# Stage borders of a two-block fp32 network: half of the second weights split before the squares of x, and a K half of the first block computed by kinds of product

## The reference, cut to what matters

```python
def _rms_norm(x, g):
    y = x * lax.rsqrt(jnp.mean(x * x, axis=-1, keepdims=True) + EPS)
    return y * g
def _swiglu(x, w_gate, w_up, w_down):
    return (jax.nn.silu(x @ w_gate) * (x @ w_up)) @ w_down
def first_block(x, ...):
    for layer in range(2):
        hf = _swiglu(_rms_norm(x, g[0]), w_gate[layer, 0], w_up[layer, 0], w_down[layer, 0])
        x = x + 0.5 * _rms_norm(hf, g[1])
        mix = (_attn_mixer, _mlstm_mixer)[layer](_rms_norm(x, g[2]), ...)
        x = x + _rms_norm(mix, g[3])
        hf = _swiglu(_rms_norm(x, g[4]), w_gate[layer, 1], w_up[layer, 1], w_down[layer, 1])
        x = x + 0.5 * _rms_norm(hf, g[5])
    return x
def second_block(x, ...):
    for l in range(2):
        p = rms_norm(x, norm_g[l]) @ w_in[l]            # 1024 x 8776
        ...                                             # conv, sparse attention, pooling branches
        merged = g0 * y_a + g1 * y_b + g2 * y_c
        x = x + merged @ w_o[l]
    return x
```

## Time and profile before

| | |
|---|---|
| median of 3 runs | 1619.91 us (1619.64 to 1620.86) |
| the profiled execution, its time | 1618.21 us |
| its span in the trace | 1616.3 us |
| PE busy | 1573.8 us, 97% |
| DVE busy | 984.2 us, 61% |
| ACT busy | 815.7 us, 50% |
| granted TensorE clock | 1.0 of full speed |

### The profile page before, as it was taken

One profiled execution on the slowest core, in us unless ns is written; L12 is line 12 of the kernel. 1 busy time (PEld: TensorE's weight loads), 2 busy tenths in 40 slices (PEclk: granted clock), 3 DMA queues, 4 the chain that ended last, 5 costly groups with the idle time before them and its releaser, 6 DMA issues.

```text
span 1616.3 us, 19404 instructions
## 1 busy us (share of the span) xinstructions
PE 1573.8 (97%) x7499; PEld 1294.7 (80%) x7499; DVE 984.2 (61%) x1247; ACT 815.7 (50%) x1023; POOL 56.6 (3%) x99
## 2 busy tenths in 40 slices
PE   7999999899999999999999999999999999999999
PEld 6888877678888888887887888887778888777887
DVE  4555567765545654467666555557956665795664
ACT  5444456354444544357666444465365446636542
POOL 2000010000000000000000000011000000100000
PEclk9999999999999999999999999999999999999999
DMA  9654763155546554564436544664434456442443
GB/s 289 211 177 144 250 208 116 53 181 196 182 143 222 203 173 156 182 223 157 151 123 208 169 168 144 227 220 168 157 104 157 158 188 231 166 156 105 157 159 128
DMA packets 189093, 279.23 MB, mean 173 GB/s; under 512 B 8509, under 2 KB 102885, under 8 KB 189024
## 3 DMA queue, kind: packets, MB, share of 16 engines
q1 hardware_dynamic: 186752, 271.27, 48.4%
q0 software_dynamic: 2128, 6.97, 1.6%
q10 hardware_dynamic: 144, 0.03, 0.0%
HBM read 277.20 MB, written 1.06 MB: 172 GB/s over the span
## 4 chain that ended last, share of the span: by engine, by line
PE 71%; DVE 16%; ACT 7%; issue 3%; DMA 2%; POOL 0%; POOLq 0%; SPq 0%; DVEq 0%; ACTq 0%
PE ACC L778 20%; PE ACC L780 19%; PE ACC L779 19%; DVE WL L1984 6%; ACT WH L1348 2%; PE TB L809 2%; DVE WL L2293 1%; PE ZB L943 1%; DVE YC L2305 1%; DMA RAW<-ffn_w_down_in 1%; ACT XH L1379 1%; PE ACC L973 1%; PE ACC L975 1%; PE ACC L974 1%; DVE IS L2512 1%
## 5 line engine op out<-in xcount | busy, mean ns | idle before, releaser
L1984 DVE TENSOR_TENSOR WL<-RAW,WH 128x2048 fp32r<-128x2048 f32 (+2 forms) x256 | 507.7, 2026 | 262.8 <-ACT WH L1348 262.8
L778 PE MATMUL ACC<-WL,XH 128*128 128x512 f32 (+2 forms) x1312 | 516.2, 393 | 10.1 <-DVE WL L1984 5.3
L780 PE MATMUL ACC<-WH,XL 128*128 128x512 f32 (+2 forms) x1312 | 507.0, 386 | 0.0
L779 PE MATMUL ACC<-WH,XH 128*128 128x512 f32 (+2 forms) x1312 | 506.3, 386 | 0.0
L1348 ACT ACTIVATE WH<-RAW 128x2048 fp32r<-128x2048 f32 (+2 forms) x256 | 421.9, 1698 | 143.2 <-PE ACC L780 95.9
L778 PEld LDWEIGHTS ACC<-WL,XH 128*128 128x128 f32 x1312 | 247.1, 188 | 67.7 <-issue 9.6
L780 PEld LDWEIGHTS ACC<-WH,XL 128*128 128x128 f32 x1312 | 247.0, 188 | 50.6
L779 PEld LDWEIGHTS ACC<-WH,XH 128*128 128x128 f32 x1312 | 247.4, 189 | 46.3
L778 PE MATMUL ACC<-WL,HH 128*128 128x512 f32 x352 | 138.4, 393 | 1.4 <-DVE WL L1984 0.9
L780 PE MATMUL ACC<-WH,HL 128*128 128x512 f32 x352 | 137.1, 390 | 0.0
L779 PE MATMUL ACC<-WH,HH 128*128 128x512 f32 x352 | 137.1, 389 | 0.0
(11 more groups left out here) (316 smaller groups left out, 1807.1 us busy)
## 6 DMA issues: line engine op xcount, KB each, us to landing
RAW<-w_in_in SPq DMA_DIRECT2D x66, 1024.0 KB, 6.9
RAW<-ffn_w_gate_in SPq DMA_DIRECT2D x43, 1024.0 KB, 5.2
RAW<-ffn_w_up_in SPq DMA_DIRECT2D x43, 1024.0 KB, 7.4
RAW<-ffn_w_down_in SPq DMA_DIRECT2D x32, 512.0 KB, 4.5
RAW<-ffn_w_down_in SPq DMA_DIRECT2D x16, 1024.0 KB, 6.7
RAW<-mlstm_w_in_in SPq DMA_DIRECT2D x16, 1024.0 KB, 6.5
RAW<-ffn_w_down_in SPq DMA_DIRECT2D x16, 768.0 KB, 6.0
RAW<-attn_w_in_in SPq DMA_DIRECT2D x12, 1024.0 KB, 7.1
```

The source lines that it names most:

```text
L778: nc.tensor.matmul(bank, lh, wl[:, i, :], start=first and i == 0, stop=False)
L779: nc.tensor.matmul(bank, lh, wh[:, i, :], start=False, stop=False)
L780: mm = nc.tensor.matmul(bank, ll, wh[:, i, :], start=False, stop=last and i == k - 1)
L1984: nc.vector.tensor_tensor(WL[:, slot, lo:hi], RAW[:, slot, lo:hi], WH[:, slot, lo:hi].bitcast(F32), ALU.subtract).then_inc(lo_ready, 1)
```

## The change

Three edits. First, on PE, in the first block of every stage but the first, token tile 0: the second K half (K tiles 4 to 7) is no longer done K tile by K tile, but as four products `XH` by `WH`, then four `XH` by `WL`, then four `XL` by `WH`. Each kind has its own wait: `groups_hi` and `hi_ready`, then `lo_ready`, then `groups_used`. The transposes of token tile 1 now stand ahead of the last four. Second, on ACT, in every stage but the first, the first half of `WH` of the second chunk is made ahead of the squares and the second half right behind them; the table load of attn and mlstm comes after both, and the gate weights of mlstm ahead of all. Third, on DVE in attn, the copy to `BROW` goes ahead of `WL` of the second chunk. `at.rounded` on PE only counts groups for the new wait.

The diff, without the hunks that only add to `at.rounded` or only pass the new argument:

```diff
--- before.py
+++ after.py
@@ -759,7 +759,8 @@
                 wl = WL[:, slot, 0:k * n].rearrange("p (k n) -> p k n", k=k)
                 for tok in range(NTOK):
                     bank = acc_of(tok) if acc_of else ACC[:, block_odd * 2 + tok, 0:n]
-                    for i in range(k):
+                    high_first = fresh is not None and tok == 0 and at.stage > 0
+                    for i in range(k // 2 if high_first else k):
                         if fresh is not None and tok == 0 and i == k - 3:
                             of_x(1, fresh + 2)
                         if fresh is not None and i in (0, k // 2):
@@ -778,6 +779,20 @@
                         nc.tensor.matmul(bank, lh, wl[:, i, :], start=first and i == 0, stop=False)
                         nc.tensor.matmul(bank, lh, wh[:, i, :], start=False, stop=False)
                         mm = nc.tensor.matmul(bank, ll, wh[:, i, :], start=False, stop=last and i == k - 1)
+                    if high_first:
+                        t = slice(0, P)
+                        pe.wait_ge(hi_ready, 2 * chunk + 2)
+                        pe.wait_ge(groups_hi, at.rounded + 2)
+                        for i in range(k // 2, k):
+                            nc.tensor.matmul(bank, xh[:, i, t], wh[:, i, :], start=False, stop=False)
+                        pe.wait_ge(lo_ready, 2 * chunk + 2)
+                        for i in range(k // 2, k):
+                            nc.tensor.matmul(bank, xh[:, i, t], wl[:, i, :], start=False, stop=False)
+                        pe.wait_ge(groups_used, fresh + 3)
+                        for i in range(k // 2, k):
+                            if i == k - 4:
+                                of_x(1, fresh + 2)
+                            mm = nc.tensor.matmul(bank, xl[:, i, t], wh[:, i, :], start=False, stop=i == k - 1)
                     if tok == 0:
                         if last:
                             mm.then_inc(tile0_ready, 1)
@@ -826,6 +841,7 @@
                 product(XH, XL, at.chunk, at.chunk % 2, at.block, at.block % 2, 0, KD, n, True, True,
                         between=between, fresh=t)
                 at.group += 4
+                at.rounded += 4
                 at.stage += 1
             def next_x():
...
@@ -1338,19 +1358,19 @@
         def _(act):
             at = At()
-            def split_hi(c, slot, raw_wait, size):
+            def split_hi(c, slot, raw_wait, size, parts=(0, 1)):
                 k, n = size
-                act.wait_ge(raw_ready[slot], raw_wait)
-                if not (isinstance(c, int) and c == 0):
+                if 0 in parts:
+                    act.wait_ge(raw_ready[slot], raw_wait)
                     act.wait_ge(weights_used, c)
-                for lo, hi in ((0, k // 2 * n), (k // 2 * n, k * n)):
+                for lo, hi in [(part * (k // 2) * n, (part + 1) * (k // 2) * n) for part in parts]:
                     nc.scalar.activation(WH[:, slot, lo:hi], RAW[:, slot, lo:hi], ACT.Copy).then_inc(hi_ready, 1)
-            def split_next(size):
+            def split_next(size, parts=(0, 1)):
                 c = at.chunk + 1
                 if size:
-                    split_hi(c, c % 2, raw_value(c), size)
+                    split_hi(c, c % 2, raw_value(c), size, parts)
             def group_hi(bank_odd, ready, dst):
                 act.wait_ge(groups_ready, ready)
@@ -1381,7 +1401,7 @@
                     ins.then_inc(groups_hi, 1)
                     at.group += 1
-            def prenorm():
+            def prenorm(next_size, between=None):
                 if at.stage == 0:
                     for q in range(FIRST_PARTS):
@@ -1395,8 +1415,13 @@
                         nc.scalar.activation(WH[:, 0, cols], RAW[:, 0, cols], ACT.Copy)\
                             .then_inc(hi_ready if q % 2 else first_hi, 1)
                 x_hi(1)
+                if between:
+                    between()
+                ahead = (0,) if at.stage else ()
+                split_next(next_size, ahead)
                 for tok in range(NTOK):
                     square(X[:, tok, :], ST[:, :, :].rearrange("p t c -> p (t c)"), tok, 1)
+                split_next(next_size, (1,) if ahead else (0, 1))
                 at.stage += 1
                 at.rsqrt += 1
...
@@ -1502,9 +1526,8 @@
                 at.rsqrt += 2
             def attn(layer, next_size):
-                prenorm()
+                prenorm(FULL)
                 act.preload_act_table_set("natural_log_exp_and_others")
-                split_next(FULL)
                 wait_rx()
                 c0, b0, u0, g0 = at.chunk, at.block, at.unit, at.group + 1
                 staged_before = {1: 0, 3: 1, 4: 3}
@@ -1570,12 +1593,13 @@
                 out_product()
             def mlstm(layer, next_size):
-                prenorm()
+                def gate_hi():
+                    act.wait_ge(gate_weights, 16)
+                    nc.scalar.activation(GWH[:, :, :], GWR[:, :, :], ACT.Copy).then_inc(gate_weights_hi, 1)
+
+                prenorm(FULL, gate_hi)
                 act.preload_act_table_set("natural_log_exp_and_others")
                 at.ln += 1
-                act.wait_ge(gate_weights, 16)
-                nc.scalar.activation(GWH[:, :, :], GWR[:, :, :], ACT.Copy).then_inc(gate_weights_hi, 1)
-                split_next(FULL)
                 wait_rx()
                 c0, b0, u0, g0 = at.chunk, at.block, at.unit, at.group
                 staged_before = {1: 0, 3: 1, 4: 3}
@@ -1789,7 +1813,8 @@
                     at.block += 2
                 for b, kind in enumerate(ORDER):
-                    split_next(SIZES[b + 1])
+                    if b:
+                        split_next(SIZES[b + 1])
                     if kind == "out":
                         activations((2, 3))
                         out_tail()
@@ -2187,11 +2212,11 @@
             def attn(layer, next_size):
                 nc.vector.memset(VS[:, :, :, :, DH:DH + 1], 1.0)
                 prenorm()
-                split_next(FULL)
                 dve.wait_ge(groups_ready, at.group + 1)
                 nc.vector.tensor_copy(BROW[:, :], TB[at.group % 2][0:HEADS, 0:3 * P]).then_inc(bias_rows, 1)
                 dve.wait_ge(bias_rows, 1)
                 dve.sem_inc(groups_used, 1)
+                split_next(FULL)
                 c0, u0, g0 = at.chunk, at.unit, at.group + 1
                 def lo(j, half):
```

More of the change, by code:

```diff
@@ L894, in ffn @@
                 at.group += NGU
+                at.rounded += NGU
                 last_hidden = lambda: hidden((t0 + NGU - 1) % 2, t0 + NGU - 1, b0 + NGU - 1)
@@ L1047, in attn @@
                 at.unit += 2 * HEADS
+                at.rounded += KD // 2
                 at.chunk += 8
@@ L1696, in mix2 @@
             def mix2(layer, next_size):
-                prenorm()
+                prenorm(SIZES[1])
                 def skip(n):
```

## The result

| | before | with the change |
|---|---|---|
| median of 14 runs each | 1620.45 us (1619.52 to 1622.99) | 1623.85 us (1622.34 to 1625.03) |
| ratio of the runs, 95% interval | | 1.0020 (1.0013 to 1.0028) |
| the profiled execution | 1618.21 us, span 1616.3 us | 1623.34 us, span 1621.6 us |

The changed kernel is slower, by 3.2 us on the ratio (2.1 to 4.5). The forecast was +1.6 us: the right side, at half of the size. The median lies inside the wide range (1618.2 to 1624.4), but above the 1620.0 to 1623.1 that the forecast had called its own (0.5 us of that is the base, 1620.45 where 1619.91 had been shown). And 0.20% is just the bound of what it called no change. No work came in: each engine has as many instructions as in rows 1, and PE is busy for 1575.0 us, 1.2 us more, in a span that is 5.3 us longer. The rest is time in which PE stands.

What follows compares the result with a forecast made beforehand. PE, busy 97% of the span, was taken as the bound, with only 42.5 us of stops to win back. Seven border terms from -0.7 to +1.15 us summed to +1.6: 1619.9 + 1.6 = 1621.5 us, range 1618.2 to 1624.4.

Steps and rivals of the forecast that it cites:

- the sign and its reason: Five borders out of ffn or mix2: transposes five products later, so token tile 1 comes 1.15 us later; total +1.6 us.
- the order by kinds: attn to ffn and mlstm to ffn: 1.4 us of stops (0.98 + 0.42) move behind the transposes instead of going away.
- the half ahead of the squares: Second chunk's first `WL` half no longer ends a wait: -0.7 us at attn to ffn and mlstm to ffn, +0.44 at ffn to ffn.
- The cover of the second half: attn to ffn: second `WL` half ready on DVE at 354.2, needed at 354.7, a cover of 0.5 us.
- the bound that I had put at the end of its range: ffn to attn: forecast -0.5 us, bounded by -1.7 if all of 1.17 + 0.57 us came back.
- the step for mix2: Borders into mix2: `WL` of chunk 1 0.95 us later delays chunk 3's load; +1.05 us from ffn, +0.85 from mix2.
- the loads of mix2 slip more: Chunk 3, both mix2 stages: `WL` 2 us later, landing slips 2.85 us each, 1625.3 us; chance 0.12 with other lost covers.
- Two of the signs: In mix2, block 3 late by over 1.5 us would show it wrong; no `WL` stop starting any second block, right.
- the sharing of the loads: Borders into mix2: chunk 4's load shares the engines with chunk 3's, so chunk 3's landing slips by 0.75 us.
- my formula: Loads in mix2: a landing slips by twice its own delay less the other's, 2 x 0.95 - 1.15 = 0.75 us.
- Free transposes: Rival, at the borders: moved transposes cost nothing and all stops go, 5.8 us, giving 1614.1 us; chance 0.06.
- Absorbed in mix2: Rival: DVE stops PE again in mix2, the last two borders' +1.9 us goes, sum -0.3, 1619.6 us; chance 0.14.

Runs made afterwards that it cites:

- the split alone: Only the ACT and DVE edits (half of `WH` ahead of the squares, `BROW` ahead of `WL`), PE's order as before, against the kernel before: 1618.01 us, ratio 0.9985.
- the second profile: The kernel before, unchanged, profiled once more: 1621.2 us.
- the next: ACT and DVE edits with PE's order as before, DVE's wait for `RX` in mix2 behind the `WL` split of chunk 1, against the kernel before: 1615.03 us, ratio 0.9966.

## Why the prediction was right, and where it was not

**Right: the sign and its reason.** At four borders `XL` of token tile 1 already ended the wait, so moving the transposes by five products had to be paid. 1.15 us was forecast. The transposes come 1.10 us later at ffn to ffn, and the PE edit alone costs 1.13 to 1.19 us at four of the five borders and 0.99 at the last.

**Right: the order by kinds wins nothing** at attn to ffn and mlstm to ffn; at attn to ffn the stops of 0.98 and 0.42 us became 0.60 and 0.82.

**Right, a little small: the half ahead of the squares.** -0.92 and -0.77 against -0.7 forecast, +0.38 against +0.44. The cover of the second half (0.5 us) held in these stages. At ffn to attn it is -0.49 against -0.5: the split alone gives -1.70 there, the bound that I had put at the end of its range, and the transposes take 1.2 of it.

**Wrong: the step for mix2.** I had written that `WL` of chunk 1 waits for "a half of `WH` behind the squares: I get 0.95 later", and of `RX` that it is ready later but "still ahead of the take-out". The second was read on ACT only. DVE in mix2 has `wait_rx()` ahead of its first split (L2594 of the kernel before), which ffn and mlstm have behind theirs and attn does not have. In the kernel before this wait cost nothing, by 0.1 us: `RX` was complete at 1058.54, the first half of `WH` at 1058.64, and `WL` started at 1058.78. That is 0.14 us behind `WH`, as the view says; where `WH` alone holds it, with the `RX` wait moved, it starts 0.10 to 0.16 us behind. With half of `WH` ahead of the squares that half is early, and `RX` is late and takes its place.

The step counted the half of `WH` and put the wait for `RX` at nothing. With that wait moved behind, `WL` of chunk 1 is complete 0.79 and 0.78 us later than before, so the 0.95 was nearly right for what it counted. With the wait where it is, the delay was 2.26 and 2.18 us: 1.1 for the transposes and 1.1 for the half of `WH` that now stands ahead of the squares, from which `RX` is made. The two terms of the sum were 1.05 and 0.85 and measured 2.89 (2.03 against the second profile) and 2.07. That covers the gap between +1.6 and the measured time; the other five terms came out 0.34 us lower than forecast.

This is the place and nearly the slip of the rival "the loads of mix2 slip more", which had 0.12 and gave another reason, squares and read-outs ahead of the second half on ACT. The chances had "no change" and "slower" parted at 0.2%, and the result lies on that line.

Two of the signs failed as well. Block 3 of a mix2 stage was late by over 1.5 us, which I had named as a sign of being wrong, and `WL` stops PE at the start of a second block, in mix2, where I had said that nowhere would. So that the time fell inside the wide range is in part luck: the range had been stretched for ffn to attn and for the product order, and not for this.

**Wrong: the sharing of the loads.** With a slip of 2.2 for chunk 3 and 1.1 for chunk 4 my formula gives 2 x 2.2 - 1.1 = 3.3 us; chunk 3 came 2.09 us later at the last border, its own slip. From `WL` of chunk 1 complete to `WH` of chunk 3 it took 8.9 us in the kernel before, with chunk 4's load 3.5 us behind, 8.8 in the changed one (2.4 behind), 9.2 with the `RX` wait behind the split (3.9), 8.9 in the next (3.9), all at the last border. By the formula 2.4 behind should have taken 1.1 us longer than 3.5 behind. At ffn to mix2 the same stretch took 8.05 and 8.90 us in two executions of the kernel before, both with the next load 3.5 us behind, so that spread is not sharing either.

The Trainium skill (DMA: Bandwidth & Descriptors, "Queues, rings and completion order") says that each DMA engine takes the descriptors of a ring in order. The times at the last border, 8.8 to 9.2 us whatever the distance, agree with that.

The 2.9 MB that had passed by the time ACT started on chunk 3 were read wrongly as sharing. At the last border 304 GB/s over the first 7.07 us behind the release make 2.15 MB in the kernel before, and 306 GB/s over 7.04 us as much in the changed one: so the size of chunk 3 had passed in equal time. ACT started 1.8 us after that in both; what makes up these 1.8 us no run here settles.

**The rivals.** Free transposes: refuted by the PE edit alone. Absorbed in mix2: refuted, the stop at 1149.28 is there in the changed kernel too, 1.34 us long at 1149.67, and comes 2.86 us later behind the border's transposes, with everything else.

**The base.** The first profiled execution of the kernel before is the only one of the ten profiled without a fall of the clock; the forecast was put on the median, so this cost nothing.

## What to carry to other kernels

When a result comes later, list every engine that waits for it, and read what is queued behind each wait, also on engines that do not use it until much later: here a wait that had 0.1 us to spare in the kernel before came to hold a weight split, and with it a load, once the work ahead of it was moved. Where transposes, evacuation and subtraction form a chain that ends just when PE needs it, PE's products ahead of the chain's start are on the path, and those behind it are free. Measure stages from border to border in both traces; it separated seven small terms of both signs that the total could not show. And where the clock fell, find a stretch between two fixed stops that no edit touches, and take out what it has grown.

## What the hardware showed that was not expected

The granted clock fell to 0.50 right behind, or at the end of, a stop of PE of about 2.75 us in 13 of 20 cases (two such stops in each of ten profiles), and not in the other seven, with stops of the same length. It cost 1.3 to 1.7 us each, and 2.7 to 2.8 us where it lasted twice as long. Once, in the second profile of the kernel before, it also fell at attn to ffn, where PE stood for 0.5 us between 336 and 340 us of that trace and for 0.9 between 340 and 343. The first profiles of both kernels have stops as long in all there, 1.40 and 1.42 us, and no fall. So these runs do not show what length of stop is safe. The fall makes a single profile of either kernel good to about 3 us only. And from the release of its wait to ACT's start a load of 2.1 MB took 8.05 to 9.2 us where ACT waited for it. That time did not follow the distance to the next load on the same queue (2.3 to 3.9 us); at ffn to mix2 it differed by 0.85 us between two executions of the same kernel.
